# The end of a decoder layer: the second half of the embedding gate's weights is rounded in two pieces, in another order among its neighbours

## The chip, the core and the metric

The kernel runs on one core of a Trainium2 chip. The metric is device time in microseconds (us), the median of several executions. A profiled execution gives the trace: instructions of TensorE (PE, its weight loads as PEld), VectorE (DVE), ScalarE (ACT), GpSimd (POOL) and the queue of SyncE (SP), from which most DMAs are issued. Its span, from the first to the last instruction, is a little shorter than the device time of the same execution.

## The reference, cut to what matters

One layer of a hybrid decoder: two mixers (a gated MLP over chunks and windowed attention), a mixture of 32 experts of which each token takes 4, and an embedding that is added through a gate. There are 512 prompt tokens and 8 sampled ones, 1024 wide.

```python
def layer_forward(h, ple, ...):
    ...
    h = h + mix
    h = h + moe(rmsnorm(h, g_moe)...)          # top 4 of 32 experts
    gate = jax.nn.sigmoid(rmsnorm(h, g_ple) @ w_ple_gate)
    h = h + gate * (ple @ w_ple_proj)
    return h, ...

y = rmsnorm(h, g_final)
```

Inside `moe`, an expert's rows are `clamped_swiglu(xb @ w_gu[e] + b_gu[e]) @ w_dn[e] + b_dn[e]`, and a token's output is the sum of its four rows, each times its gate. `w_ple_gate` is 1024 x 1024, `w_ple_proj` 256 x 1024.

## The kernel before

**Tiles.** Tokens are worked in five tiles: tiles 0 to 3 have 128 prompt tokens each, tile 4 the 8 sampled ones. All products take FP32 operands as a rounded part ("hi") and its remainder ("lo"): hi x hi, hi x lo and lo x hi are summed in a PSUM bank. ScalarE makes the hi part, VectorE the lo part. The eight PSUM banks are `bank[:, 0]` to `bank[:, 7]`.

**Experts.** A loop runs over blocks of up to 128 tokens of one expert; there are 32 blocks, and one more for each time an expert has over 128 tokens (`n_extra`, worked out from the count of tokens for each expert, `total`, line 1541). POOL gathers a block's token rows, ScalarE and VectorE split twelve pieces of weights of 1 MB each, TensorE multiplies, and ScalarE copies the block's output from PSUM into the one buffer `y_sb` (`y_out`, line 1152), from which POOL scatters it to rows in HBM (`store`, line 865). A scatter must have landed before the next `y_out` may write `y_sb`.

**The end.** After the last block (nb - 1) the program is written out by hand, each engine with its own list in order, held together by semaphores:

- `turn_inputs(t)` (PE, L2221, L2224) turns the gate table and the embedding input of tile t; `inputs(t)` copies them out on ACT (L1213, L1214) and DVE (L1692).
- `down_bias(t)` (PE, L2235) multiplies the gates by the experts' output biases into banks 4 and 5; `add_bias(t)` (DVE, L1701) adds them to the residual `h_in`. The two banks are the same for every tile, so `down_bias(t)` waits for `add_bias(t - 1)`.
- `project(t)` (PE, L78 with `wp_hi`, `wp_lo`) is the embedding's projection into banks 6 and 7; `embedding(t)` (ACT, L1220) copies it out. `project(t)` waits for `embedding(t - 1)`.
- `add_experts(t)` (DVE, L1713) adds the four expert rows of each token, which SP loads into `y_in` (L738, L739, L743) once the last scatter has landed. It signals `moe_ready`.
- `turn_f(t)` (PE, L2262) waits for `moe_ready` and turns the tile; `f_hi` (ACT, L1238) and `f_lo` (DVE, L1727) split it; `gate_product(t, w)` (PE, L78 with `wg_hi`, `wg_lo`) multiplies it by half w of the gate's weights; then follow the sigmoid, the embedding and the last norm.
- The gate's weights come in two halves w = 0, 1 of 1024 x 512. `gate_hi(w)` (ACT, L1273) scales and rounds a half in eight instructions, one for each chunk of 128 rows; `split_gate(w)` (DVE, L1753) forms the remainders in eight instructions. `raw` holds the loaded weights.

What TensorE does at the end is, in this order: `turn_inputs` 0 and 1, the last block's down product, then `down_bias(0)`, `turn_inputs` 2 and 3, `project(0)`, `down_bias(1)`, `turn_inputs(4)`, `project(1)`, `down_bias(2)`, `project(2)`, `down_bias(3)`, `project(3)`, `turn_f(0)`, `down_bias(4)`, `project(4)`, and from there for each tile the two gate products with the next tile's `turn_f` between them.

Of the kernel before, what the change touches and what calls it, by code (L numbers as in the profile page):

```python
# [72 lines left out]
def product(nc, out, x_hi, x_lo, w_hi, w_lo, chunks, cols, start, stop):  # L73


    for i, (cx, cw) in enumerate(chunks):
        for j, (a, b) in enumerate(((x_hi, w_hi), (x_hi, w_lo), (x_lo, w_hi))):
            last = nc.tensor.matmul(out, a(cx), b[:, cw, 0:cols], start=start and i == 0 and j == 0,  # L78
                                    stop=stop and i == len(chunks) - 1 and j == 2)
    return last  # L80


def hybrid_layer(nc, x_prompt, x_sample, cache_k, cache_v, p_prompt, p_sample, g_mix, w_in, ln_v_g,
# [10 lines left out]
    KC = D // P  # L94
    HALFK = KC // 2
# [8 lines left out]
    E = w_router.shape[2]  # L104
# [39 lines left out]
    def sem(name):  # L144
        return ctx.enter_context(nc.semaphore(name))
# [9 lines left out]
    bank = ctx.enter_context(nc.psum_tensor("bank", [P, 8, 512], F32))  # L155
# [161 lines left out]
    def scratch(name, shape, dt=F32):  # L317
        nonlocal o
        size = 4
        for n in shape[1:]:  # L320
            size *= n
        t = at(name, shape, dt, o)
        o += -(-size // 32) * 32
        return t
# [89 lines left out]
    total = scratch("total", [P, E])  # L414
# [133 lines left out]
    def piece(b, k):  # L548
        return k if isinstance(b, int) and b == 0 else 12 * b - 4 + k
# [53 lines left out]
    wg_hi_ready, wg_lo_ready, h_biased, emb_ready = sem("wg_hi_ready"), sem("wg_lo_ready"), sem("h_biased"), sem("emb_ready")  # L603
# [8 lines left out]
    def two_banks(b, R):  # L612
        return bank[0:R, b:b + 2, :].rearrange("p b n -> p (b n)")
# [11 lines left out]
    with nc.Block() as block:  # L625
# [263 lines left out]
        def _(act):  # L889
            mine = act_steps.on(act)  # L890
# [255 lines left out]
            def y_out(b, done, first_bank=4):  # L1146

                act.wait_ge(half_used, done)
                if not isinstance(b, int) or b >= 1:
                    act.wait_ge(y_stored, 16 * b)  # L1150
                for s in range(2):
                    last = nc.scalar.activation(y_sb[:, s * CB:(s + 1) * CB], bank[:, first_bank + s, :], ACT.Copy)  # L1152
                last.then_inc(y_ready, 1)
# [51 lines left out]
            def inputs(t):  # L1205

                R, i = ROWS[t], t % NT
                act.wait_ge(turned_in, t + 1)
                if t == NT:
                    act.wait_ge(bdn_done, 1)  # L1210
                    act.wait_ge(ple_proj_done, 1)
                b = bank[:, 2 + t % 2, :]
                nc.scalar.activation(gT[i][:, 0:R], b[0:E, 0:R], ACT.Copy)  # L1213
                nc.scalar.activation(pT_hi[i][:, :, 0:R], b[:, P:P + PC * R].rearrange("p (c r) -> p c r", c=PC),  # L1214
                                     ACT.Copy).then_inc(turned_read, 1)

            def embedding(t):
                R = ROWS[t]
                act.wait_ge(ple_proj_done, t + 1)
                nc.scalar.activation(emb[0:R, t, :], two_banks(6, R), ACT.Copy).then_inc(emb_ready, 1)  # L1220
# [42 lines left out]
                mine.settle()  # L1263
                mine(nc.scalar.activation(st[:, 2:3], st[:, 2:3], ACT.Sqrt, scale=1.0 / D, bias=EPS), out_ss)

            def gate_hi(w):

                if w == 0:
                    act.wait_ge(gain_landed, 80)
                act.wait_ge(raw_landed[w], 48)  # L1270
                act.wait_ge(lo_ready, piece(nb, 1) + 1)
                for c in range(KC):
                    last = nc.scalar.activation(wg_hi[w][:, c, :], raw[w][:, c, :], ACT.Copy, scale=gain_pT[:, c:c + 1])  # L1273
                last.then_inc(wg_hi_ready, 1)

# [2 lines left out]
            y_out(nb - 2, piece(nb - 1, 11) + 1)  # L1278
            act.wait_ge(raw_landed[2], 32)
            nc.scalar.activation(wp_hi[:], wp_raw[:], ACT.Copy).then_inc(wg_hi_ready, 1)  # L1280
            gate_hi(0)
            y_out(nb - 1, piece(nb, 3) + 1, 0)
            inputs(2)
            inputs(3)
            embedding(0)
            gate_hi(1)
            embedding(1)
            inputs(4)
            embedding(2)
            embedding(3)  # L1290
            f_hi(0)
# [12 lines left out]
        def _(dve):  # L1304
            mine = dve_steps.on(dve)
# [232 lines left out]
                                         ALU.subtract), gate_in)  # L1538

            dve.wait_ge(count_done, 1)  # L1540
            mine(nc.vector.tensor_copy(total[:], bank[:, 6, 0:E]))
            mine.settle()
            mine(nc.vector.tensor_scalar(extra[0][:], total[:], float(P), None, ALU.is_gt))
            for j in range(2, -(-TOK // P)):
# [38 lines left out]
            mine = loop_steps  # L1583
# [62 lines left out]
            mine = dve_steps.on(dve)  # L1646
# [13 lines left out]
            mine = loop_steps  # L1660
# [24 lines left out]
            mine = dve_steps.on(dve)  # L1685

            def inputs(t):
                R, i = ROWS[t], t % NT
                dve.wait_ge(turned_read, t + 1)
                if t == NT:  # L1690
                    dve.wait_ge(ple_proj_done, 1)
                mine(nc.vector.tensor_tensor(pT_lo[i][:, :, 0:R],  # L1692
                                             bank[:, 2 + t % 2, P:P + PC * R].rearrange("p (c r) -> p c r", c=PC),
                                             pT_hi[i][:, :, 0:R].bitcast(F32), ALU.subtract), pT_lo_ready)

            def add_bias(t):
                R = ROWS[t]
                if t == 0:
                    dve.wait_ge(h_in_landed, 32)
                dve.wait_ge(bdn_done, t + 1)  # L1700
                mine(nc.vector.tensor_tensor(h_in[0:R, t, :], h_in[0:R, t, :], two_banks(4, R), ALU.add), h_biased)  # L1701
# [44 lines left out]
                mine.settle()  # L1746
                mine(nc.vector.scalar_tensor_tensor(h, h, st[:, 3:4], gain_f[0:R, :], ALU.mult, ALU.mult), y_final)

            def split_gate(w):

                dve.wait_ge(wg_hi_ready, w + 2)
                for c in range(KC):
                    last = nc.vector.scalar_tensor_tensor(wg_lo[w][:, c, :], raw[w][:, c, :], gain_pT[:, c:c + 1],  # L1753
                                                          wg_hi[w][:, c, :].bitcast(F32), ALU.mult, ALU.subtract)
                mine(last, wg_lo_ready)
# [2 lines left out]
            inputs(1)  # L1758
            dve.wait_ge(wg_hi_ready, 1)
            mine(nc.vector.tensor_tensor(wp_lo[:], wp_raw[:], wp_hi[:].bitcast(F32), ALU.subtract), wg_lo_ready)  # L1760
            split_gate(0)
            add_bias(0)
            inputs(2)
            inputs(3)
            add_bias(1)
            inputs(4)
            split_gate(1)
            add_bias(2)
            add_experts(0)
            add_bias(3)  # L1770
# [16 lines left out]
        def _(pe):  # L1787
# [478 lines left out]
            def gate_product(t, w):  # L2266
                if w == 0:
                    pe.wait_ge(fT_hi_ready, t + 1)
                    pe.wait_ge(fT_lo_ready, t + 1)
                    if t == 0:  # L2270
                        pe.wait_ge(y_ready, nb)
                    elif t == 1:
                        pe.wait_ge(h_biased, TILES)
                    else:
                        pe.wait_ge(sg_ready, t - 1)
                if t == 0:
                    pe.wait_ge(wg_lo_ready, w + 2)
                product(nc, bank[:, 4 * (t % 2) + w, :], lambda c: fT_hi[t % 2][:, c, :], lambda c: fT_lo[t % 2][:, c, :],
                        wg_hi[w], wg_lo[w], [(k, k) for k in range(KC)], CB, True, True).then_inc(ple_gate_done, 1)

# [18 lines left out]
            for t in range(TILES):  # L2299
                gate_product(t, 0)  # L2300
                if t + 1 < TILES:
                    turn_f(t + 1)
                gate_product(t, 1)
# [39 lines left out]
```

## Time and profile before

| | us |
|---|---|
| median of 3 runs | 1534.76 (1534.58 to 1535.76) |
| profiled execution | 1534.55 |
| its span | 1533.2 |
| PE busy | 1472.7 (96%) |
| DVE busy | 1229.0 (80%) |
| ACT busy | 1040.3 (68%) |
| POOL busy | 187.5 (12%) |

The shares of busy time are means over the whole span, in which the loop over the experts takes most of the time. The end of the program, from about 1420 us on, has an order and limits of its own; there the rows of a timeline, which give the start and length of each step and the idle time ahead of it, tell more than the shares. Steps of one engine overlap in the rows by up to 0.1 us, as an instruction is counted until its write is through.

### The profile page before, as it was taken

How to read it: one execution, taken by the hardware profiler on the slowest of the kernel's cores; microseconds unless marked ns; L12 is line 12 of the kernel's file. 1: busy time of each engine (PE TensorE's matmuls, PEld its weight loads, DVE VectorE, ACT ScalarE, POOL GpSimd, SP SyncE). 2: the span in 40 equal slices, each digit the busy share in tenths (PEclk: the TensorE clock that was granted, in tenths of full speed). 3: DMA queues.
4: the chain of work that ended last, by engine and by line, in shares of the span. 5: the costliest groups of instructions: out<-in, count | busy, mean ns of one | idle time of the engine just before them, and what ended most of it. 6: DMA issues, size and time to landing. Idle time of an engine off the chain costs nothing.

```text
span 1533.2 us, 21023 instructions
## 1 busy us (share of the span) xinstructions
PE 1472.7 (96%) x6907; PEld 1205.8 (79%) x6907; DVE 1229.0 (80%) x1031; ACT 1040.3 (68%) x980; POOL 187.5 (12%) x237
## 2 busy tenths in 40 slices
PE   5999996799999999999999999999999999999898
PEld 5878775578888888888888888888888888888576
DVE  4246745698888888888888888888888888888775
ACT  4467512377777777777777777777777777777645
POOL 6000013101111111101111111110111111110000
PEclk8999998799999999999999999999999999999999
DMA  9013423899999999999999999999999999998531
GB/s 324 23 65 101 165 84 139 340 338 364 370 368 359 374 366 366 368 368 362 381 375 356 360 367 367 362 362 375 361 379 358 377 356 383 366 360 290 206 127 43
DMA packets 108568, 465.89 MB, mean 304 GB/s; under 512 B 19082, under 2 KB 24722, under 8 KB 75770
## 3 DMA queue, kind: packets, MB, share of 16 engines
q1 hardware_dynamic: 93482, 445.24, 76.6%
q0 software_dynamic: 14432, 18.94, 3.5%
q10 hardware_dynamic: 624, 1.31, 0.3%
q8 instruction: 18, 0.29, 0.1%
q14 instruction: 12, 0.10, 0.0%
HBM read 457.50 MB, written 24.96 MB: 315 GB/s over the span
## 4 chain that ended last, share of the span: by engine, by line
PE 88%; DMA 4%; DVE 3%; ACT 2%; SPq 2%; issue 1%; POOL 0%; POOLq 0%; ACTq 0%; DVEq 0%
PE bank L2151 31%; PE bank L2154 15%; PE bank L2172 15%; PE bank L78 10%; PE bank L2177 7%; PE bank L2143 2%; PE bank L2122 2%; PE bank L2133 2%; DMA v_win<-v_nat 2%; SPq L647 1%; DMA uq<-in_x_prompt 1%; PE bank L1877 1%; PE bank L1847 1%; DMA w_slot<-in_w_dn 1%; PE bank L2069 0%
## 5 line engine op out<-in xcount | busy, mean ns | idle before, releaser
L1588 DVE TENSOR_TENSOR pair_lo<-w_slot,pair_hi 128x2048 fp32r<-128x2048 f32 x384 | 871.3, 2291 | 130.1 <-ACT pair_hi L1123 130.0
L1123 ACT ACTIVATE pair_hi<-w_slot 128x2048 fp32r<-128x2048 f32 x384 | 737.2, 1921 | 268.4 <-PE bank L2154 191.6
L2151 PE MATMUL bank<-pair_hi,xg_hi 128*128 128x512 f32 x1024 | 279.5, 395 | 0.5 <-issue 0.5
L2151 PE MATMUL bank<-pair_hi,xg_lo 128*128 128x512 f32 x1024 | 275.2, 391 | 0.0
L2154 PE MATMUL bank<-pair_lo,xg_hi 128*128 128x512 f32 x1024 | 274.1, 389 | 0.0
L2151 PEld LDWEIGHTS bank<-pair_hi,xg_hi 128*128 128x128 f32 x1024 | 190.7, 189 | 50.8 <-issue 12.8
L2151 PEld LDWEIGHTS bank<-pair_hi,xg_lo 128*128 128x128 f32 x1024 | 193.4, 189 | 40.7
L2154 PEld LDWEIGHTS bank<-pair_lo,xg_hi 128*128 128x128 f32 x1024 | 192.5, 188 | 40.1
L2172 PE MATMUL bank<-pair_hi,aT_hi 128*128 128x512 f32 x496 | 135.7, 395 | 0.0
L2177 PE MATMUL bank<-pair_lo,aT_hi 128*128 128x512 f32 x496 | 133.0, 390 | 0.0
L2172 PE MATMUL bank<-pair_hi,aT_lo 128*128 128x512 f32 x496 | 132.9, 390 | 0.0
L2177 PEld LDWEIGHTS bank<-pair_lo,aT_hi 128*128 128x128 f32 x496 | 93.1, 188 | 20.0
L2172 PEld LDWEIGHTS bank<-pair_hi,aT_lo 128*128 128x128 f32 x496 | 93.1, 188 | 19.9
L2172 PEld LDWEIGHTS bank<-pair_hi,aT_hi 128*128 128x128 f32 x496 | 90.8, 188 | 17.0
L78 PE MATMUL bank<-half_hi,xT_hi 128*128 128x512 f32 (+1 forms) x220 | 86.3, 392 | 4.6 <-DVE half_lo L254 2.8
L78 PE MATMUL bank<-half_hi,xT_lo 128*128 128x512 f32 (+1 forms) x220 | 83.0, 377 | 0.0
L78 PE MATMUL bank<-half_lo,xT_hi 128*128 128x512 f32 (+1 forms) x220 | 82.9, 377 | 0.0
L846 POOL DMA_INDIRECT xg<-hn_rows,idx_in x33 | 37.0, 1120 | 320.9 <-PE bank L2122 283.3
L865 POOL DMA_INDIRECT expert_rows<-y_sb,idx_out x32 | 44.2, 1382 | 210.5 <-ACT y_sb L1152 137.3
L1144 ACT ACTIVATE gate_sb<-bank 128x512 f32<-128x512 f32 x64 | 34.8, 596 | 35.1 <-PE bank L2154 35.1
L855 POOL DMA_DIRECT2D bias_sb<-bias_rows x32 | 19.7, 614 | 289.9 <-issue 252.7
L78 PEld LDWEIGHTS bank<-half_hi,xT_hi 128*128 128x128 f32 x220 | 42.3, 192 | 14.1 <-issue 3.9
(305 smaller groups left out, 1460.7 us busy)
## 6 DMA issues: line engine op xcount, KB each, us to landing
w_slot<-in_w_gu SPq DMA_DIRECT2D x256, 1024.0 KB, 6.5
w_slot<-in_w_dn SPq DMA_DIRECT2D x128, 1024.0 KB, 6.1
raw<-in_w_in SPq DMA_DIRECT2D x3, 2048.0 KB, 22.8
y_in<-expert_rows SPq DMA_DIRECT2D x3, 2048.0 KB, 10.1
raw<-in_w_o SPq DMA_DIRECT2D x2, 2048.0 KB, 8.7
raw<-in_w_ple_gate SPq DMA_DIRECT2D x2, 2048.0 KB, 10.9
uq<-in_x_prompt SPq DMA_DIRECT2D x4, 512.0 KB, 7.7
x_rows<-in_x_prompt SPq DMA_DIRECT2D x4, 512.0 KB, 6.8
```

The lines of the kernel that those rows point to most:

```text
L78: last = nc.tensor.matmul(out, a(cx), b[:, cw, 0:cols], start=start and i == 0 and j == 0, stop=stop and i == len(chunks) - 1 and j == 2)
L846: pool.indirect_dma_start(xg[:], None, hn_rows, bass.IndirectOffsetOnAxis(idx_in[:, 0:1], 0), bounds_check=last_token, oob_is_err=False).t ...
L865: pool.indirect_dma_start(expert_rows, bass.IndirectOffsetOnAxis(idx_out[:, 1:2], 0), y_sb[:], None, bounds_check=last_row, oob_is_err=Fal ...
L1123: nc.scalar.activation(pair_hi[pair(b, k)][:], w_slot[k + down][:], ACT.Copy).then_inc(hi_ready, 1)
L1144: nc.scalar.activation(gate_sb[:, p * CB:(p + 1) * CB], bank[:, p, :], ACT.Gelu_apprx_sigmoid).then_inc(gate_ready, 1)
L1588: mine(nc.vector.tensor_tensor(pair_lo[pair(b, k)][:], w_slot[k + down][:], pair_hi[pair(b, k)][:].bitcast(F32), ALU.subtract), lo_ready)
L2122: last = nc.tensor.transpose(bank[:, 6 + c // 4, (c % 4) * P:(c % 4 + 1) * P], xg[:, c * P:(c + 1) * P], ident[:])
L2133: last = nc.tensor.transpose(bank[:, 6 + p, c * P:(c + 1) * P], acts[:, p * CB + c * P:p * CB + (c + 1) * P], ident[:])
L2151: nc.tensor.matmul(bank[:, n, :], x[:, c, :], w_hi[:, n * CB:(n + 1) * CB], start=False, stop=False)
L2154: last = nc.tensor.matmul(bank[:, n, :], xg_hi[:, c, :], w_lo[:, n * CB:(n + 1) * CB], start=False, stop=c == KC - 1)
L2172: nc.tensor.matmul(bank[:, first_bank + s, :], a[:, 2 * j + i, :], w_hi[:, i * D + s * CB:i * D + (s + 1) * CB], start=j == 0 and i == 0 a ...
L2177: last = nc.tensor.matmul(bank[:, first_bank + s, :], aT[0][:, 2 * j + i, :], w_lo[:, i * D + s * CB:i * D + (s + 1) * CB], start=False, s ...
```

## The change

The second half of the gate's weights (w = 1) is rounded, and its remainders are formed, in two pieces of four chunks each. On ScalarE the first piece stands ahead of the copy of the last block's rows (`y_out(nb - 1)`) and the second behind `inputs(3)`; `inputs(4)` goes ahead of `embedding(1)`. On VectorE the first piece stands ahead of `add_bias(1)` and the second behind it, so that `add_bias(2)` and `add_experts(0)` follow `inputs(4)`. The semaphore `wg_lo_ready` counts one more step, which the gate's product waits for. Besides, the count of tokens for each expert is read from bank 1, into which TensorE writes it (`positions`), instead of bank 6, in which the last tile's router logits stand.

```diff
-            def gate_hi(w):
+            def gate_hi(w, chunks):
...
-                for c in range(KC):
+                for c in chunks:
                     last = nc.scalar.activation(wg_hi[w][:, c, :], raw[w][:, c, :], ACT.Copy, scale=gain_pT[:, c:c + 1])
                 last.then_inc(wg_hi_ready, 1)
...
-            gate_hi(0)
+            gate_hi(0, range(KC))
+            gate_hi(1, range(HALFK))
             y_out(nb - 1, piece(nb, 3) + 1, 0)
             inputs(2)
             inputs(3)
+            gate_hi(1, range(HALFK, KC))
             embedding(0)
-            gate_hi(1)
+            inputs(4)
             embedding(1)
-            inputs(4)
             embedding(2)
...
-            mine(nc.vector.tensor_copy(total[:], bank[:, 6, 0:E]))
+            mine(nc.vector.tensor_copy(total[:], bank[:, 1, 0:E]))
...
-                dve.wait_ge(wg_hi_ready, w + 2)
-                for c in range(KC):
+                dve.wait_ge(wg_hi_ready, w + 1 + chunks.stop // HALFK if w else 2)
+                for c in chunks:
...
-            split_gate(0)
+            split_gate(0, range(KC))
             add_bias(0)
             inputs(2)
             inputs(3)
+            split_gate(1, range(HALFK))
             add_bias(1)
+            split_gate(1, range(HALFK, KC))
             inputs(4)
-            split_gate(1)
             add_bias(2)
...
-                    pe.wait_ge(wg_lo_ready, w + 2)
+                    pe.wait_ge(wg_lo_ready, 2 * w + 2)
```

How the program's instructions stand on ScalarE between the rounding of the first half (`wg_hi_190`, eight chunks of `raw_49`) and the first tile's `f_hi` (`fT_hi_208`), before (-) and now (+); `wg_hi_191` is the second half, `y_sb` the copy of the last rows, `gT` and `pT_hi` are the inputs, `emb` the projections:

```order
 L1273 ACTIVATE wg_hi_190<-raw_49,gain_pT 128x512 x8
+L1273 ACTIVATE wg_hi_191<-raw_50,gain_pT 128x512 x4
 L1150 REGISTER_ALU
 L1152 ACTIVATE y_sb<-bank 128x512 x2
...
 L1213 ACTIVATE gT_223<-bank 32x128
 L1214 ACTIVATE pT_hi_215<-bank 128x256
-L1220 ACTIVATE emb<-bank 128x1024
-L1273 ACTIVATE wg_hi_191<-raw_50,gain_pT 128x512 x8
+L1273 ACTIVATE wg_hi_191<-raw_50,gain_pT 128x512 x4
 L1220 ACTIVATE emb<-bank 128x1024
 L1213 ACTIVATE gT_220<-bank 32x8
 L1214 ACTIVATE pT_hi_212<-bank 128x2x8
-L1220 ACTIVATE emb<-bank 128x1024 x2
+L1220 ACTIVATE emb<-bank 128x1024 x3
```

Four of the eight roundings of the second half now stand ahead of the copy into `y_sb`, four ahead of the first `emb`, and the inputs of tile 4 stand behind one `emb` instead of two.

VectorE before, from the remainders of the first half (`wg_lo_192`) to the bias sum of tile 3; `h_in<-h_in,bank` is `add_bias`, `pT_lo` the inputs, `h_in<-y_in_202,gates,h_in` `add_experts(0)`:

```order
L1753 SCALAR_TENSOR_TENSOR wg_lo_192<-raw_49,gain_pT,wg_hi_190 128x512 x8
L1701 TENSOR_TENSOR h_in<-h_in,bank 128x1024
L1692 TENSOR_TENSOR pT_lo_218<-bank,pT_hi_214 128x256
L1692 TENSOR_TENSOR pT_lo_219<-bank,pT_hi_215 128x256
L1701 TENSOR_TENSOR h_in<-h_in,bank 128x1024
L1692 TENSOR_TENSOR pT_lo_216<-bank,pT_hi_212 128x2x8
L1753 SCALAR_TENSOR_TENSOR wg_lo_193<-raw_50,gain_pT,wg_hi_191 128x512 x8
L1701 TENSOR_TENSOR h_in<-h_in,bank 128x1024
L1713 SCALAR_TENSOR_TENSOR h_in<-y_in_202,gates,h_in 128x1024 x4
L1701 TENSOR_TENSOR h_in<-h_in,bank 128x1024
```

The same stretch of VectorE now (the lines of this half of the program are numbered one higher):

```order
L1754 SCALAR_TENSOR_TENSOR wg_lo_192<-raw_49,gain_pT,wg_hi_190 128x512 x8
L1702 TENSOR_TENSOR h_in<-h_in,bank 128x1024
L1693 TENSOR_TENSOR pT_lo_218<-bank,pT_hi_214 128x256
L1693 TENSOR_TENSOR pT_lo_219<-bank,pT_hi_215 128x256
L1754 SCALAR_TENSOR_TENSOR wg_lo_193<-raw_50,gain_pT,wg_hi_191 128x512 x4
L1702 TENSOR_TENSOR h_in<-h_in,bank 128x1024
L1754 SCALAR_TENSOR_TENSOR wg_lo_193<-raw_50,gain_pT,wg_hi_191 128x512 x4
L1693 TENSOR_TENSOR pT_lo_216<-bank,pT_hi_212 128x2x8
L1702 TENSOR_TENSOR h_in<-h_in,bank 128x1024
L1714 SCALAR_TENSOR_TENSOR h_in<-y_in_202,gates,h_in 128x1024 x4
L1702 TENSOR_TENSOR h_in<-h_in,bank 128x1024
```

The eight remainders of the second half stood between `add_bias(1)` and `add_bias(2)`, behind the inputs of tile 4; now four stand ahead of `add_bias(1)` and four directly behind it.

## Rows read from the trace of the kernel before

**Rows 1.** The page: the span and the count of instructions.
```profile
span 1533.2 us, 21023 instructions
```

**Rows 2.** Busy us by stretch; its length, busy (x instructions), granted clock, DMA share, GB/s.
```profile
1422.00:1448.60 26.60, 26.48 (x105) 18.28 (x105) 18.51 (x23) 18.78 (x34) 2.72 (x3) 1.00 0.53 194
1448.60:1452.30 3.70, 0.00 (x0) 0.00 (x0) 3.62 (x5) 1.02 (x1) 0.00 (x0) 0.86 1.02 414
1452.30:1461.50 9.20, 9.14 (x17) 5.36 (x18) 6.27 (x5) 0.00 (x0) 0.00 (x0) 0.50 0.31 108
1473.70:1525.60 51.90, 51.85 (x243) 42.59 (x241) 35.62 (x42) 29.77 (x47) 0.00 (x0) 1.00 0.21 80
```

**Rows 3.** Chain that ended last, from 1439 us: start, length, what (merged pieces).
```profile
1439.56 4.13 ACT wg_hi L1273 x7
...
1445.79 5.30 DVE wg_lo L1753 x8
1451.09 1.14 DVE h_in L1701
...
1456.11 5.43 PE bank L78 x12
```

**Rows 4.** Timeline of TensorE: start, length, instruction xcount, [idle before <-releaser].
```profile
1433.10 1.98 PE L2235 MATMUL bank<-b_down,gT 32*128 32x512 f32 x4
1435.01 0.28 PE L2221 MATMUL bank<-ident,gate_table 128*32 128x128 f32 x1
...
1435.59 0.47 PE L78 MATMUL bank<-wp_hi,pT_hi 128*128 128x512 f32 x1
...
1438.53 1.98 PE L2235 MATMUL bank<-b_down,gT 32*128 32x512 f32 x4
...
1443.54 1.98 PE L2235 MATMUL bank<-b_down,gT 32*128 32x512 f32 x4
...
1452.36 3.75 PE L2235 MATMUL bank<-b_down,gT 32*128 32x512 f32 x4 [3.78 <-DVE h_in L1701]
...
1461.33 1.14 PE L2262 MATMUL bank<-ident,h_in 128*128 128x128 f32 x8
...
1472.85 1.10 PE L2262 MATMUL bank<-ident,h_in 128*128 128x128 f32 x8 [0.19 <-DVE h_in L1713]
```

**Rows 5.** Timeline of ScalarE: first half rounded, last rows' copy, end of inputs(3).
```profile
1426.79 5.00 ACT L1273 ACTIVATE wg_hi<-raw,gain_pT 128x512 fp32r<-128x512 f32 x8
1434.23 1.09 ACT L1152 ACTIVATE y_sb<-bank 128x512 f32<-128x512 f32 x2 [2.44 <-DMA expert_rows<-y_sb,idx_out]
...
1436.14 0.36 ACT L1214 ACTIVATE pT_hi<-bank 128x256 fp32r<-128x256 f32 x1
```

**Rows 6.** Timeline of GpSimd: the last block's index rows and scatter.
```profile
1434.86 0.55 POOL L860 DMA_DIRECT2D idx_out<-slot_table  x1 [7.81 <-DMA expert_rows<-y_sb,idx_out]
1437.62 1.02 POOL L865 DMA_INDIRECT expert_rows<-y_sb,idx_out  x1 [2.21 <-DMA idx_out<-slot_table]
```

**Rows 7.** Timeline of VectorE from the first half's remainders on.
```profile
1431.82 5.39 DVE L1753 SCALAR_TENSOR_TENSOR wg_lo<-raw,gain_pT,wg_hi 128x512 fp32r<-128x512 f32 x8 [2.61 <-ACT wg_hi L1273]
1437.13 1.22 DVE L1701 TENSOR_TENSOR h_in<-h_in,bank 128x1024 f32<-128x1024 f32 x1
1438.26 0.75 DVE L1692 TENSOR_TENSOR pT_lo<-bank,pT_hi 128x256 fp32r<-128x256 f32 x2
...
1452.32 5.31 DVE L1713 SCALAR_TENSOR_TENSOR h_in<-y_in,gates,h_in 128x1024 f32<-128x1024 f32 x4
```

**Rows 8.** DMA issues from 1440.89, 1441.82 and 1391.3 us: xcount, KB, us to landing.
```profile
y_in<-expert_rows SPq DMA_DIRECT2D x1, 1024.0 KB, 5.4
...
y_in<-expert_rows SPq DMA_DIRECT2D x1, 2048.0 KB, 12.1
...
raw<-in_w_ple_gate SPq DMA_DIRECT2D x1, 2048.0 KB, 13.3
```

**Rows 9.** Line 865, all scatters: shortest/median/longest ns, first and last start us.
```profile
L865 POOL DMA_INDIRECT expert_rows<-y_sb,idx_out x32: 1021/1512/2788, 350.6 to 1437.6; - x32
```

More of the change, by code:

```diff
@@ L1747, in norm_out, with split_gate @@
                 mine(nc.vector.scalar_tensor_tensor(h, h, st[:, 3:4], gain_f[0:R, :], ALU.mult, ALU.mult), y_final)
-            def split_gate(w):
-                dve.wait_ge(wg_hi_ready, w + 2)
-                for c in range(KC):
+            def split_gate(w, chunks):
+                dve.wait_ge(wg_hi_ready, w + 1 + chunks.stop // HALFK if w else 2)
+                for c in chunks:
                     last = nc.vector.scalar_tensor_tensor(wg_lo[w][:, c, :], raw[w][:, c, :], gain_pT[:, c:c + 1],
```

## The prediction

> **What bounds the kernel now.** Read the page first: a span of 1533.2 us [rows 1], of which the loop over the experts is the largest part. The diff leaves that loop alone; it works on the last 100 us, so the views to read are those of the stretch from 1422 us. The table by stretch [rows 2] shows TensorE busy for 26.48 of 26.60 us up to 1448.6, then not at all for 3.70 us, then busy at a granted clock of 0.50, which is 1.2 GHz, for 9.2 us, and from 1473.7 on busy for 51.85 of 51.90 us at 1.00 (2.4 GHz). So the end is one long TensorE chain with a single hole in it, and behind the hole a slow stretch. Whatever removes the hole moves everything behind it, since the five gate products that follow have no room left between them.
>
> What made the hole stands in the chain of waits [rows 3]: ScalarE rounds the second half of the gate's weights (wg_hi, 4.13 us of it on the chain), VectorE forms their remainders in one run of eight (5.30 us), then the bias sum of tile 2 (1.14 us), and only then TensorE may start down_bias(3), whose two banks that sum has to empty first. TensorE's rows say the same: down_bias(3) starts at 1452.36 after 3.78 us of idling for VectorE's h_in [rows 4]. Nobody on TensorE needs these remainders then; the first user is gate_product(0, 1), behind turn_f(1) at 1472.85 [rows 4]. They are merely queued in front of add_bias(2).
>
> **The change part by part.**
>
> *ScalarE, first piece ahead of the last rows' copy.* Eight roundings take 5.00 us [rows 5], so four take 2.5. They start where the eight of the first half end, at 1431.79 or up to 0.1 before it (neighbours overlap that much in the rows), and end near 1434.25. The copy y_out(nb - 1) has its idle time of 2.44 us exactly there, and starts at 1434.23 because the rows before it leave y_sb only then [rows 5]. So the copy is late by 0 to 0.1 us. What if it were later? Behind it stands POOL's scatter, which also waits for its index rows: these are asked for at 1434.86, and POOL then idles 2.21 us for them until the scatter goes at 1437.62 [rows 6]. The copy takes 1.09 us and ends at 1435.32, so up to 2.3 us of delay reach nobody. The weights themselves landed 13.3 us after an issue before 1392 [rows 8], so this piece waits for no transfer. Cost: nothing.
>
> *ScalarE, second piece behind inputs(3).* inputs(3) ends at 1436.50; four roundings end near 1438.95, and embedding(0), for which project(0) is done at 1435.59 + 2.94 = 1438.5 [rows 4], comes 0.3 us later than now, ending near 1439.9. project(1) needs it; it starts at about 1440.5, behind down_bias(1) (1438.53 + 1.98) and the last transposes [rows 4]. 0.6 us of room: nothing. In return embedding(1) no longer stands behind eight roundings and inputs(4) no longer behind embedding(1).
>
> *VectorE.* It is busy without a gap from 1431.82, so its steps can be laid end to end, with durations from [rows 7]: the eight remainders of the first half end at 1437.2, add_bias(0) at 1438.35, inputs(2) and inputs(3) at 1439.0. Now four remainders: 5.39 us for eight, so 2.7 for four, to 1441.7; add_bias(1) (1.22 less 0.1 of overlap) to 1442.8; four more to 1445.5; the small inputs(4) to 1445.6; add_bias(2) to 1446.8, against 1452.2; add_experts(0), 5.31 us, to 1452.1, against 1457.6; add_bias(3) to 1453.3.
>
> Two of these release TensorE at another time than now. add_bias(1) is later by some of the four remainders ahead of it, and down_bias(2) waits for it; that starts at 1443.54 [rows 4], so 0.7 us of room are left: nothing. add_bias(2) is 5.4 us earlier (1452.23 now [rows 3]), and down_bias(3) finds its banks empty when project(2) is done.
>
> *TensorE.* The hole goes. From 1443.54 the steps follow each other at full clock: down_bias takes 1.91 us to the next step's start (1433.10 to 1435.01), a projection 2.94 us (1435.59 to 1438.53) [rows 4], 4.85 together. So turn_f(0), two such pairs behind 1443.54, starts at 1453.24. It starts at 1461.33 now [rows 4]. The gain is 8.09 us: 3.8 of idling, the rest the half clock over down_bias(3) (3.75 us against 1.98) and project(3) (5.43 us against 2.94) [rows 3, 4]. The slowest reading of the rows is the pair from 1438.53 to 1443.54, 5.01 us, which has the small transposes in it; by it the gain is 7.77.
>
> *Who is late next?* turn_f(0) also needs moe_ready, the end of add_experts(0) at 1452.1: 1.1 us of room. That step in turn needs the gathered rows, which used to be there long before. Their first megabyte lands 5.4 us after 1440.89, at 1446.3, and it is wanted at 1446.8. The last of the three transfers in the queue lands 12.1 us after 1441.82, at 1453.9 [rows 8]. The second megabyte is not seen landing; as 1 of the 3 MB that come between 1446.3 and 1453.9 it should land near 1448.8 if the queue keeps its order, and it is wanted by the third sum, near 1449.4. If the two transfers in the queue shared evenly, it would land near 1451.5, add_experts(0) would end at 1454.1 and turn_f(0) would lose 0.9. I take the order of the queue, since the first landing agrees with it, and keep 7.2 as the lower end of the gain.
>
> *The rest* (the gate's product waits for semaphore value 4 instead of 3, the count is read from bank 1) is one instruction for one instruction. From turn_f(0) on, ScalarE's and VectorE's steps all hang on project(3) and turn_f(0) and move with them; the gate products are bound by TensorE [rows 2], and so the end moves by the same 8.1 us.
>
> *A rule of the Trainium skill.* Its page "GPSIMD Engine Reference" (1. Specifications) says that GpSimd's SBUF interfaces are shared with VectorE, and that they collide with VectorE instructions that have two SBUF inputs; the remainders are such instructions. In this trace the scatters of expert rows took 1.02 to 2.79 us [rows 9], and the last one, beside add_bias(0), 1.02 [rows 6]. If the last scatter fell into the moved remainders and took the longest of these times, the rows would land 1.8 us later, add_experts(0) would end near 1453.4, and the sum would be 7.9 instead of 8.1. The remainders start at 1439.0 and the scatter is issued by 1438.64, so I leave it out.
>
> **The rivals.**
>
> *The rows come too late.* The room of 1.1 us in front of turn_f(0) is what the forecast lives on. If the gathered rows come d us later than laid out, d - 1.1 is lost; and if the new hole grows to some 3.7 us, the clock falls again and the following 9 us run at half speed, as they do now. Then the hole has only moved behind project(3). Time: between 1527 and 1534.5. For it: the second megabyte's landing was not seen. Against it: the first was, in time, and nothing ahead of it moves.
>
> *The clock falls anyway.* If the half clock at 1452 came not from the hole but from the light work before it (small transposes, products over 32 rows), the hole would go and the slow stretch stay: gain 3.8, time 1531.0. Against it: that same light work ran at 1.00 from 1433 to 1448.6 [rows 2], and the clock was lower only behind the hole.
>
> *Nothing reaches the end.* This needs a second bound behind the hole, as late as the first. The rows show a TensorE chain without a gap behind 1473.7, so little speaks for it: 1533.5 to 1535.
>
> *Slower: another expert block.* The count of tokens for each expert was read from a bank in which the logits stand; read from the bank with the counts, it can exceed 128. From one expert with 129 tokens on, the loop runs a 33rd time. A block costs (1437.6 - 350.6) / 31 = 35.1 us [rows 9], so the time would be 1534.8 + 35.1 - 8.1 = 1561.8. Against it: 520 tokens in four choices over 32 experts are 65 for each on average, and the reference's own routing, worked out for its inputs, gives at most 117.
>
> **How the numbers follow.** The profiled execution took 1534.55 us, 0.2 below the median of 1534.76. 1534.76 - 8.1 = 1526.66. Chances: the forecast (1525.8 to 1527.8) 0.80; rows too late 0.09, half of it within 2.5 us of the forecast; clock falls anyway 0.04; nothing reaches the end 0.04; slower block or anything else that costs 0.03. The range from 1525.7 to 1529.2 takes in the lower end of the gain (7.2, so 1527.6) and the smaller part of the first rival. A measurement of this kernel tells 0.2% (3.1 us) from no change. By that: faster 0.91, same 0.06, slower 0.03.
>
> **What would show it.** Right: TensorE without a hole at 1448 to 1453, granted clock 1.00 from 1422 to the end of the products, add_bias(2) ending near 1446.8, turn_f(0) near 1453.2, the last gate product ending near 1517.5, and y_out still near 1434.3 with its idle time gone. Wrong: idle time of TensorE in front of turn_f(0) or project(1), VectorE waiting for y_in inside add_experts(0), the last scatter later than 1438, or 33 blocks.

## The result, and the profile after

| | before | changed |
|---|---|---|
| median, us | 1534.58 (5 runs, 1533.39 to 1535.76) | 1526.15 (5 runs, 1525.64 to 1526.72) |
| ratio | | 0.9945, 95% interval 0.993 to 0.9959 |
| profiled execution, us | 1534.55 | 1526.72 |
| its span, us | 1533.2 | 1525.3 |

8.4 us less (0.55%; the interval reaches from 6.3 to 10.7), where 8.1 were forecast.

The part ahead of the change differs from execution to execution: the first multiplication of the last block's down product starts between 1421.0 and 1427.0 us in the profiles of this study, all of them with the same program up to there except for the bank that the count is read from. So beside the times each kernel is read by its **end stretch**, from that multiplication to the end of the span: 111.2 us before (from 1422.00), 102.9 changed (from 1422.37), 8.3 us less. An end stretch is that of one profiled execution; the times are those of all executions and contain the part ahead. The changed kernel's rows stand 0.37 us later than those of before from this alone.

The stretches of the changed kernel (columns as in [rows 2]: busy us of TensorE, its weight loads, VectorE, ScalarE, GpSimd; the hole and the slow stretch behind it have no counterpart any more):

```profile
1422.00:1448.60 26.60, 26.23 (x105) 18.31 (x105) 23.72 (x30) 19.13 (x34) 2.71 (x3) 1.00 0.50 183
1448.60:1453.30 4.70, 4.70 (x17) 2.84 (x16) 4.56 (x4) 1.02 (x1) 0.00 (x0) 1.00 0.99 403
1453.30:1465.40 12.10, 11.88 (x54) 8.29 (x53) 8.10 (x9) 5.96 (x9) 0.00 (x0) 1.00 0.48 178
1465.40:1517.60 52.20, 52.20 (x247) 43.08 (x245) 35.52 (x41) 30.19 (x46) 0.00 (x0) 1.00 0.20 78
```

TensorE's granted clock is 1.00 (2.4 GHz) throughout. It is busy but for 0.37 us at the start of the first row, where this execution is not yet at its down product, and 0.22 us in front of turn_f(1). The hole and the 9.2 us at 0.50 are gone. In the chain of waits (start, length, what) the pieces of ScalarE and VectorE of [rows 3] have gone with them; up to turn_f(0) the pairs of bias product and projection stand end to end:

```profile
1443.98 1.91 PE bank L2237 x4
1445.89 2.95 PE bank L78 x12
1448.84 1.91 PE bank L2237 x4
1450.75 2.97 PE bank L78 x12
```

VectorE (beside [rows 7]): the four remainders, add_bias(2), add_experts(0), add_bias(3) follow each other without a wait.

```profile
1443.08 2.74 DVE L1754 SCALAR_TENSOR_TENSOR wg_lo<-raw,gain_pT,wg_hi 128x512 fp32r<-128x512 f32 x4
...
1445.93 1.22 DVE L1702 TENSOR_TENSOR h_in<-h_in,bank 128x1024 f32<-128x1024 f32 x1
1447.25 5.32 DVE L1714 SCALAR_TENSOR_TENSOR h_in<-y_in,gates,h_in 128x1024 f32<-128x1024 f32 x4
1452.48 1.22 DVE L1702 TENSOR_TENSOR h_in<-h_in,bank 128x1024 f32<-128x1024 f32 x1
```

ScalarE (beside [rows 5]): twelve roundings in a row, and 0.36 us of the 2.44 are left in front of the copy, since the rows before it left `y_sb` a little later in this execution.

```profile
1427.17 7.45 ACT L1273 ACTIVATE wg_hi<-raw,gain_pT 128x512 fp32r<-128x512 f32 x12
1434.98 1.08 ACT L1152 ACTIVATE y_sb<-bank 128x512 f32<-128x512 f32 x2 [0.36 <-DMA expert_rows<-y_sb,idx_out]
```

GpSimd's last scatter, then TensorE's turn_f(0) and turn_f(1) (beside [rows 4, 6]):

```profile
1438.37 1.02 POOL L865 DMA_INDIRECT expert_rows<-y_sb,idx_out  x1 [2.21 <-DMA idx_out<-slot_table]
```
```profile
1453.54 1.04 PE L2264 MATMUL bank<-ident,h_in 128*128 128x128 f32 x8
...
1465.00 1.09 PE L2264 MATMUL bank<-ident,h_in 128*128 128x128 f32 x8 [0.22 <-DVE h_in L1714]
```

The scatter still waits 2.21 us for its index rows, so nothing of the moved roundings reached it. turn_f(0) follows project(3) without a wait.

### The profile page after: what moved, and what is told of

It is laid out like the page before. It is cut to its first block, busy times and chain, and to the rows that moved or that the text cites. A ratio compares the mean times of both kernels' runs of the same rounds, so it can differ in the third digit from the quotient of the medians.

```text
span 1525.3 us, 21024 instructions
## 1 busy us (share of the span) xinstructions
PE 1467.7 (96%) x6907; PEld 1204.2 (79%) x6907; DVE 1228.9 (81%) x1031; ACT 1040.3 (68%) x980; POOL 187.2 (12%) x237
## 4 chain that ended last, share of the span: by engine, by line
PE 89%; DMA 4%; DVE 3%; ACT 2%; SPq 2%; issue 1%; POOL 0%; POOLq 0%; DVEq 0%; ACTq 0%
PE bank L2153 31%; PE bank L2156 15%; PE bank L2174 15%; PE bank L78 10%; PE bank L2179 7%; PE bank L2145 2%; PE bank L2124 2%; DMA v_win<-v_nat 2%; PE bank L2135 2%; SPq L647 1%; DMA uq<-in_x_prompt 1%; PE bank L1879 1%; PE bank L1849 1%; DMA w_slot<-in_w_dn 1%; PE bank L2237 1%
## 6 DMA issues: line engine op xcount, KB each, us to landing
raw<-in_w_ple_gate SPq DMA_DIRECT2D x2, 2048.0 KB, 10.7
```

## The experiments

Theory: the gain is the hole in front of down_bias(3) and the half clock behind it, and the room of 1 us in front of turn_f(0) is what carries it. The rivals are those of the prediction, and a question it left unasked: which of the two engines' orders made the hole.

The idling in the table is TensorE's in front of a bias product or turn_f(0); the 0.2 us in front of turn_f(1), which the kernel before has too, are left out. The time at clock 0.50 is counted from the end of that idling to the last gate product.

| kernel | idling of TensorE on the way, us | at clock 0.50, us | end stretch, us | ratio to before (95%) |
|---|---|---|---|---|
| before | 3.78 | 9.2 | 111.2 | 1 |
| changed | none | none | 102.9 | 0.9945 (0.993 to 0.9959) |
| changed_again | none | none | 103.0 | 0.9952 (0.9938 to 0.9965) |
| act_only | 0.44 | 3.4 | 104.9 | 0.9954 (0.9941 to 0.9967) |
| act_only_again | 0.41 | none | 103.6 | one execution |
| dve_only | 2.55 | 3.4 | 107.1 | 0.9987 (0.9978 to 0.9996) |
| hole2 | 0.86 | 3.4 | 105.5 | 0.9969 (0.9958 to 0.998) |
| hole2_again | 0.82 | 3.4 | 105.4 | one execution |
| hole5 | 4.59 | 8.5 | 111.7 | 1.0004 (0.9993 to 1.0014) |
| count_only | 3.78 | 6.8 | 110.1 | 1.0009 (1.0 to 1.0018) |
| eight_ahead | none | none | 102.9 | 0.9961 (0.9948 to 0.9974) |
| halves_swapped | 0.91 | none | 104.1 | 0.9972 (0.9962 to 0.9983) |
| tile1_first | 3.50 | 9.4 | 110.6 | 1.0 (0.9991 to 1.0009) |
| sums_before_norm | none | none | 102.5 | 0.9946 (0.9933 to 0.996) |

### Which engine's order made the hole

`act_only`, ScalarE's order of the change with VectorE's of before:

```diff
-            split_gate(1, range(HALFK))
             add_bias(1)
-            split_gate(1, range(HALFK, KC))
             inputs(4)
+            split_gate(1, range(HALFK))
+            split_gate(1, range(HALFK, KC))
             add_bias(2)
```

> ScalarE in the order of the change, VectorE in the order of before (all eight remainders of the second half behind the inputs of tile 4, ahead of add_bias(2)). Theory A: the hole came from ScalarE, whose late rounding of the second half kept the inputs of tile 4 back, so that VectorE idled 3.85 us for them ahead of its remainders. Then VectorE now runs through: inputs(4) near 1442.2, remainders to 1447.5, add_bias(2) to 1448.7, just when TensorE is free for down_bias(3) (1448.8), so no hole and no half clock; add_experts(0) ends near 1454.1 and turn_f(0) is 0.6 us later than with the whole change: about 1526.8. Theory B: the hole came from VectorE's order, the run of eight ahead of add_bias(2). Then it stays, and the time is 1533 to 1534.6.

VectorE of `act_only` (the cut row is inputs(4)), and below it the row of the kernel before that the prediction passed over, VectorE's inputs(4):

```profile
1444.54 1.22 DVE L1702 TENSOR_TENSOR h_in<-h_in,bank 128x1024 f32<-128x1024 f32 x1 [1.55 <-PE bank L2237]
...
1445.76 5.38 DVE L1754 SCALAR_TENSOR_TENSOR wg_lo<-raw,gain_pT,wg_hi 128x512 fp32r<-128x512 f32 x8
1451.06 1.21 DVE L1702 TENSOR_TENSOR h_in<-h_in,bank 128x1024 f32<-128x1024 f32 x1
```

Before:

```profile
1445.61 0.17 DVE L1692 TENSOR_TENSOR pT_lo<-bank,pT_hi 128x16 fp32r<-128x16 f32 x1 [3.85 <-ACT pT_hi L1214]
```

Before, VectorE stood idle for 3.85 us, because inputs(4) was queued on ScalarE behind the eight roundings and embedding(1). With ScalarE's order alone that wait is gone, the run of eight remainders stays whole, and add_bias(2) ends at 1452.27, when TensorE asks for its banks at 1452.41. Theory A: the hole is gone, with 0.44 us left in front of turn_f(0). Behind these 0.44 us the profiled execution lost 1.4 us more than expected, to a half clock (below). `act_only` moves the first roundings and inputs(4) together; which of the two was needed, no run tells.

`dve_only` is the other half: VectorE's order of the change, ScalarE's of before.

```diff
-            gate_hi(1, range(HALFK))
             y_out(nb - 1, piece(nb, 3) + 1, 0)
             inputs(2)
             inputs(3)
-            gate_hi(1, range(HALFK, KC))
             embedding(0)
-            inputs(4)
+            gate_hi(1, range(HALFK))
+            gate_hi(1, range(HALFK, KC))
             embedding(1)
+            inputs(4)
```

> VectorE in the order of the change (four remainders ahead of add_bias(1), four behind it), ScalarE in the order of before (second half rounded behind embedding(0), inputs(4) behind embedding(1)). Theory A: VectorE now waits for the first four roundings until 1442.5, so add_bias(1) ends near 1446.4 and TensorE idles 2.5 us ahead of down_bias(2); add_bias(2) follows near 1450.3 without a further hole, and if 2.5 us of idling leave the clock at 1.00, turn_f(0) comes near 1456: about 1528.7. Theory B: the order on VectorE is what matters: about 1526.2.

```profile
1445.76 2.15 PE L2237 MATMUL bank<-b_down,gT 32*128 32x512 f32 x4 [2.55 <-DVE h_in L1702]
```
```profile
1441.74 2.74 DVE L1754 SCALAR_TENSOR_TENSOR wg_lo<-raw,gain_pT,wg_hi 128x512 fp32r<-128x512 f32 x4 [3.09 <-ACT wg_hi L1273]
```

TensorE's hole moved one step ahead, to down_bias(2), 2.55 us where 2.5 were forecast, because VectorE waits 3.09 us for roundings that are not there yet; another 1.6 us went to a half clock. Of the 8.3 us of the end stretch this order alone gives 4.1 in its profile, ScalarE's alone 6.3 and 7.6 in two. They are not two gains to be added: each order alone leaves a hole of its own, in another place and of another length. The times agree with this for `act_only` (7.1 us less than before, 5.1 to 9.1). For `dve_only` they are 2.0 us less (0.6 to 3.4), so its profile, the fastest of twelve executions, shows more than they do; what the others lost was not seen.

### The hole and the clock

`hole2` and `hole5` put two and five subtractions of 128x1024 ahead of add_bias(2) of the changed kernel:

```diff
             inputs(4)
+            for i in range(5):
+                mine.settle()
+                mine(nc.vector.tensor_tensor(sg[:], wg_hi[0][:, 0:2, :].bitcast(F32), wg_hi[0][:, 2:4, :].bitcast(F32), ALU.subtract))
             add_bias(2)
```

> The changed kernel with five such subtractions ahead of add_bias(2), about 6.3 us, so that TensorE idles some 4.7 us, one more than in the kernel before. Theory: the hole and the half clock belong together; down_bias(3) and project(3) run at 1.2 GHz again (9 us instead of 4.8) and turn_f(0) is about 9 us later: about 1535. Rival (the half clock of before had another cause, which the change took away): only the idling comes back and add_experts(0) decides, turn_f(0) 5.4 us later: about 1531.6, clock 1.00.

```profile
1454.53 3.75 PE L2240 MATMUL bank<-b_down,gT 32*128 32x512 f32 x4 [4.59 <-DVE h_in L1702]
```
```profile
1449.95:1454.50 4.55, 0.00 (x0) 0.00 (x0) 4.38 (x5) 1.02 (x1) 0.00 (x0) 0.82 0.88 353
1454.50:1463.20 8.70, 8.67 (x16) 5.09 (x17) 6.26 (x5) 0.00 (x0) 0.00 (x0) 0.51 0.23 73
```

A hole of the old kind brings back down_bias(3) at 3.75 us, a stretch at 0.51 and 8.8 us of the end. That the hole and the half clock belong together is shown: TensorE did the same work, in the same order, in the changed kernel at 1.00. `hole5` also gives VectorE 6 us more to do; `tile1_first` (below) makes a hole without that, and the clock falls there too.

> The changed kernel with two extra subtractions of 128x1024 on VectorE (about 1.25 us each, their output not used) ahead of add_bias(2). If idling costs only itself while it is short: TensorE idles 0.9 us ahead of down_bias(3), then add_experts(0) ends 2.5 us later, 1.5 us behind the room in front of turn_f(0): about 1527.7, granted clock 1.00 throughout. If any idling halves the clock: 1530 to 1532, with clock 0.50 behind 1450.

```profile
1450.64 1.95 PE L2240 MATMUL bank<-b_down,gT 32*128 32x512 f32 x4 [0.86 <-DVE h_in L1702]
```
```profile
1450.60:1453.00 2.40, 2.36 (x6) 1.10 (x7) 2.36 (x2) 0.25 (x1) 0.00 (x0) 0.98 1.03 413
1453.20:1456.60 3.40, 3.40 (x10) 2.68 (x9) 3.26 (x4) 0.00 (x0) 0.00 (x0) 0.54 0.31 122
1456.80:1468.40 11.60, 11.39 (x50) 7.81 (x48) 7.94 (x9) 5.54 (x9) 0.00 (x0) 1.00 0.46 182
```

The end is 2.6 us longer, not 1.5: 0.86 us of idling in front of down_bias(3), and then, 2.3 us behind it, the clock falls for 3.4 us while TensorE is busy. So a short hole costs more than its length here. Is that always so?

> The kernel with two extra subtractions ahead of add_bias(2), once more. It took 105.5 us over the end, 2.6 more than the changed kernel, with 3.4 us at 0.50 behind 0.86 us of idling. If the drop belongs to the idling: 105.5 again. If it is a matter of the execution: down to 104.4 without it.

> The kernel with only ScalarE's order changed, once more. It took 104.9 us over the end where 103.5 was expected: behind 0.44 us of idling in front of turn_f(0) the clock was 0.50 for 3.4 us. If that drop belongs to the idling, it comes again: 104.9. If a short idle time only loses the clock in some executions: 103.5 or 104.9.

`hole2_again` lost the clock again (105.4 us). `act_only_again` didn't. turn_f(0) and the stretch behind it in `act_only` and, under it, in `act_only_again`:

```profile
1457.74 1.09 PE L2264 MATMUL bank<-ident,h_in 128*128 128x128 f32 x8 [0.44 <-DVE h_in L1714]
```
```profile
1457.20:1460.80 3.60, 3.04 (x14) 1.17 (x13) 2.43 (x4) 2.95 (x5) 0.00 (x0) 0.99 0.47 135
1460.90:1464.30 3.40, 3.40 (x9) 2.68 (x10) 2.04 (x4) 1.58 (x4) 0.00 (x0) 0.53 1.01 414
```
```profile
1457.62 1.09 PE L2264 MATMUL bank<-ident,h_in 128*128 128x128 f32 x8 [0.41 <-DVE h_in L1714]
```
```profile
1457.10:1460.70 3.60, 3.06 (x14) 1.19 (x13) 2.43 (x4) 2.97 (x5) 0.00 (x0) 1.00 0.47 139
1460.80:1464.20 3.40, 3.40 (x15) 2.77 (x16) 2.04 (x4) 2.02 (x4) 0.00 (x0) 1.00 1.01 417
```

The same program, with the same idling within 0.03 us: once at 0.53 and once at 1.00 behind it. So whether a short hole in this part of TensorE's work (transposes, products over 32 rows, a projection) loses the clock differs from execution to execution, and its length alone doesn't decide it: `halves_swapped` (below) kept the clock behind 0.91 us. The idling can be counted on, the 3.4 us at half clock can't. In the four profiles without such a hole (changed, changed_again, eight_ahead, sums_before_norm) the clock stayed at 1.00 until the products were over.

### The count

`count_only` is the kernel before with the changed line of the count alone.

```diff
-            mine(nc.vector.tensor_copy(total[:], bank[:, 6, 0:E]))
+            mine(nc.vector.tensor_copy(total[:], bank[:, 1, 0:E]))
```

> The kernel before with nothing but the count of tokens read from bank 1. If no expert has over 128 tokens: 32 blocks and the time of before, within 0.7 us. If one has (the slower rival): 33 scatters and 35 us more, 1569.7.

```profile
L865 POOL DMA_INDIRECT expert_rows<-y_sb,idx_out x32: 1022/1548/3027, 352.3 to 1439.4; - x32
```

32 scatters, so 32 blocks, and a ratio of 1.0009 (1.0 to 1.0018, 0 to 2.8 us more): the slower rival's 35 us did not come about, and the line gives none of the gain. This run also shows what the half clock of before is worth from one execution to the next: behind the same hole of 3.78 us, down_bias(3) and project(3) took 8.00 us here (1453.73 to 1461.73) and 8.97 in [rows 4].

```profile
1453.73 3.71 PE L2235 MATMUL bank<-b_down,gT 32*128 32x512 f32 x4 [3.78 <-DVE h_in L1701]
```
```profile
1453.70:1461.70 8.00, 7.97 (x16) 4.55 (x17) 6.26 (x5) 0.00 (x0) 0.00 (x0) 0.57 0.28 82
```

Read in steps of 0.2 us, the clock was at 0.50 from 1453.8 to 1460.6 here, so it fell just as the hole ended; before, it fell some 1.1 us ahead of the hole's end and stayed there until 1461.5.

### The copy, the scatter and the rows

`eight_ahead` rounds the whole second half ahead of the last rows' copy.

```diff
             gate_hi(1, range(HALFK))
+            gate_hi(1, range(HALFK, KC))
             y_out(nb - 1, piece(nb, 3) + 1, 0)
             inputs(2)
             inputs(3)
-            gate_hi(1, range(HALFK, KC))
             embedding(0)
```

> The changed kernel with all eight roundings of the second half ahead of the last rows' copy. Theory: the copy is 2.1 us later (about 1437.1) and still hidden behind the index rows of the last scatter, which stays near 1438.4, so the time is that of the change, 1526.2 within 0.5. Rival (the copy is on the path to the scatter): scatter and y_in 2 us later, of which 1 us is covered ahead of turn_f(0): 1527.2 to 1528.2.

```profile
1442.14 1.02 POOL L865 DMA_INDIRECT expert_rows<-y_sb,idx_out  x1 [2.68 <-ACT y_sb L1152]
```
```profile
1442.61 2.73 DVE L1754 SCALAR_TENSOR_TENSOR wg_lo<-raw,gain_pT,wg_hi 128x512 fp32r<-128x512 f32 x4
...
1450.95 1.28 DVE L1714 SCALAR_TENSOR_TENSOR h_in<-y_in,gates,h_in 128x1024 f32<-128x1024 f32 x1 [0.49 <-DMA y_in<-expert_rows]
```

The scatter now waits for the copy instead of its index rows and is 0.45 us later against the end stretch's beginning; VectorE waits 0.49 us for the rows; turn_f(0) is where it was, and the end stretch is 102.9. So the room is there, in both places, and a little of it was used. The expectation was off by that 0.45, which it had as nothing. Its time of 1526.2 was missed as well: the median is 1529.04, beside 1534.48 for the kernel before, 6.0 us less (4.0 to 8.0), which can't be told from the changed kernel's 8.4. These rows also show the moved remainders beside the scatter, from 1442.61 to 1443.16: it took 1.02 us, as it does without them.

`halves_swapped` loads the second megabyte of tile 0's rows first.

```diff
-            sp.dma_start(y_in[0][:, 0:2, :], y_by_token[0:P, 0:2, :]).then_inc(y_first_landed, 16)
             sp.dma_start(y_in[0][:, 2:TOPK, :], y_by_token[0:P, 2:TOPK, :]).then_inc(y_in_landed[0], 16)
+            sp.dma_start(y_in[0][:, 0:2, :], y_by_token[0:P, 0:2, :]).then_inc(y_first_landed, 16)
```

> The changed kernel, with the second megabyte of the gathered rows of tile 0 loaded ahead of the first, so that the sums begin only when both are there. If the queue keeps its order: the first two rows land about 2.5 us later than now (near 1449.5 instead of 1447.05), VectorE waits 2.3 us for them, and behind 1.0 us of room turn_f(0) is 1.3 us later: about 1527.5, no half clock. If the two transfers share the queue, or the room is larger: 1526.2.

```profile
1447.93 5.31 DVE L1714 SCALAR_TENSOR_TENSOR h_in<-y_in,gates,h_in 128x1024 f32<-128x1024 f32 x4 [2.09 <-DMA y_in<-expert_rows]
```
```profile
1453.30 1.09 PE L2264 MATMUL bank<-ident,h_in 128*128 128x128 f32 x8 [0.91 <-DVE h_in L1714]
```

The second of the two transfers lands 7.1 us after its issue at 1440.78, where the first, in the changed kernel, landed after 5.4: here the transfers land one after the other, in the order of their issue. This landing comes 2.0 us behind where the first megabyte is wanted in the changed kernel. VectorE waits 2.09 us, 0.91 of it come through to turn_f(0), 1.1 us to the end. No half clock here, behind 0.91 us of idling. The timed runs lose more than this one profile (4.3 us less than before, 2.6 to 5.8, where the profile's end gives 7.1). The profiled execution was the fastest of ten, with the part ahead at its shortest (1421.04). That some of the others lost the clock, as `act_only` did once, would fit too, but was not seen; this stays open.

`tile1_first` goes further and puts tile 1's 2 MB ahead of tile 0's.

```diff
+            sp.dma_start(y_in[1][:], rows_of(y_by_token, 1)).then_inc(y_in_landed[1], 16)
             sp.dma_start(y_in[0][:, 0:2, :], y_by_token[0:P, 0:2, :]).then_inc(y_first_landed, 16)
             sp.dma_start(y_in[0][:, 2:TOPK, :], y_by_token[0:P, 2:TOPK, :]).then_inc(y_in_landed[0], 16)
-            for t in range(1, TILES):
+            for t in range(2, TILES):
```

> The changed kernel, with the 2 MB of tile 1's rows loaded ahead of tile 0's: the first rival (rows too late) on purpose. The rows of tile 0 land 5 us later, near 1452, add_experts(0) ends near 1457.4 and TensorE idles 3.9 us ahead of turn_f(0). Theory: the clock falls to 0.50 there, the hole has moved behind project(3): 1533 to 1534.4. Rival (only the idling costs): 1530.1, clock 1.00.

```profile
1456.60 1.97 PE L2265 MATMUL bank<-ident,h_in 128*128 128x128 f32 x8 [3.50 <-DVE h_in L1715]
```
```profile
1456.60:1465.60 9.00, 9.00 (x21) 4.76 (x22) 5.55 (x7) 3.61 (x6) 0.00 (x0) 0.50 0.62 233
```

The whole gain is gone (end stretch 110.6, ratio 1.0): the prediction's first rival, made on purpose, with the hole moved behind project(3) and 9.4 us at half clock behind it. Tile 0's first megabyte lands 10.3 us after its issue at 1440.94, against the end stretch's beginning 4.8 us later than in the changed kernel.

### One more move

`changed_again` repeats the changed kernel. `sums_before_norm` moves one wait more: in the changed kernel turn_f(1) idles 0.22 us for add_experts(1), which VectorE forms behind a wait for tile 0's norm.

```diff
-            norm_in(0)
             add_bias(4)
             add_experts(1)
+            norm_in(0)
```

> The changed kernel once more, beside the next three. From the first multiplication of the last block's down product to the end of the span it took 102.9 us, with the granted clock at 1.00 all the way to the last gate product. If the clock there is safe without a hole: 102.9 again within 0.3. If the light stretch from 1452 to 1460 can lose it without a hole: up to 2 us more.

> The changed kernel with one more move on VectorE: add_bias(4) and add_experts(1) go ahead of the reciprocal of tile 0's norm, for which VectorE waits 1.26 us behind ScalarE's table load; only the sigmoid, 13 us later, needs it. turn_f(1), which now idles 0.22 us for add_experts(1), then starts when TensorE is free: 102.5 to 102.7 over the end instead of 102.9. If something else holds turn_f(1): 102.9. Slower would mean that the sigmoid waits for the reciprocal.

```profile
1466.14 1.03 PE L2264 MATMUL bank<-ident,h_in 128*128 128x128 f32 x8
```

The changed kernel's end was 103.0 us again, at clock 1.00. With the move, turn_f(1) starts at 1466.14, 11.1 us behind turn_f(0) instead of 11.5, without a wait, and the end stretch is 102.5. It is the fastest of all ends here; by the times (1526.75 against 1527.64 us, side by side) 0.5 us can't be told from nothing.

## Why the prediction was right

- *The bound.* TensorE's chain with one hole and a slow stretch behind it: right; `hole5` puts both back and the 8.8 us with them.
- *The sum.* 8.09 us to turn_f(0); measured 1461.33 - 1453.54, plus the 0.37 by which this execution was late at the start, 8.16. A pair of bias product and projection took 4.86 and 4.77 us, forecast 4.85. To the end it is 8.3, since turn_f(0) itself took 1.04 us instead of 1.14. It is these rows that bear the sum out; the times alone, 8.4 us with an interval from 6.3 to 10.7, couldn't tell 8.1 from 7.
- *ScalarE's first piece at no cost.* Right; `eight_ahead` shows that 2.1 us more would have cost the scatter 0.45 and the end nothing. One sign of being wrong did come up: the last scatter started at 1438.37, later than 1438. It was not the roundings, which left 0.36 us of idling in front of the copy: of the 0.75 us by which it is later than in [rows 6], 0.37 are this execution's late start and the rest the later landing of the rows before.
- *add_bias(1) later, with 0.7 us of room.* Right, down_bias(2) came without a wait.
- *The room in front of turn_f(0).* Forecast 1.1 us; add_experts(0) ended at 1452.57 and turn_f(0) started at 1453.54, so 0.97. In front of the first sum it was less than thought: the rows landed 5.4 us after 1441.65, at 1447.05, and were wanted at 1447.25. The second megabyte, by the 7.1 us of `halves_swapped`, came at 1449.2 and was wanted at 1449.9. The order of the queue, which was taken over equal shares, held.
- *GpSimd's shared interfaces.* The rule of the Trainium skill ("GPSIMD Engine Reference", 1. Specifications) was left out of the sum. In the changed kernel the scatter ended 0.09 us after the moved remainders began, so they hardly met; in `eight_ahead` they overlapped for 0.55 us and the scatter took 1.02 us all the same, so no price of it is seen in this overlap.
- *The cause of the hole* was put in the wrong place, without harm to the sum. The prediction read it as remainders queued ahead of add_bias(2), and took VectorE as busy without a gap from 1431.82. In the kernel before it was not: it idled 1.53 us in front of add_bias(1) and 3.85 in front of inputs(4). `act_only` leaves the remainders there, and the hole is gone: the 3.85 us were VectorE's wait for inputs(4), which ScalarE had queued behind its roundings. The prediction named that move in half a sentence and gave it no price.
- *"The clock falls anyway"* had a chance of 0.04, on the ground that light work had run at 1.00. For the changed kernel that held in both its profiles. But light work behind a short hole did lose the clock in some executions (`act_only`, `hole2`), so the rival was nearer than the text had it: the changed kernel leaves no hole up to turn_f(0), and short ones there are not harmless.

## What to carry to other kernels

When an engine idles in front of the bound one, follow its own idle rows back one step further: the wait of 3.85 us on VectorE, behind work on ScalarE whose result TensorE first used 29 us later, was the root, and moving that work into idle times which other waits had already made was free. A hole on TensorE between light steps is worth closing to the end: here 0.4 to 0.9 us of it could be followed by 3.4 us at half clock (1.3 to 1.7 us more), and was in three profiles of five. Where a gain rests on a room of a microsecond, know what lands last ahead of it; here 4.8 us of delay in a queue of DMAs took the whole gain back.

## What was not expected of the hardware

- The granted clock fell from 1.00 to 0.50 for 3.4 us some 2.5 us behind an idle time of 0.82 to 0.86 us (`hole2` and `hole2_again`) and about 3 us behind one of 0.44 us (`act_only`, not `act_only_again`), while TensorE was busy with transposes, products over 32 rows and a projection; behind 0.91 us in `halves_swapped` it stayed at 1.00. Behind 2.55 us (`dve_only`) it was at 0.50 for 3.4 us. Behind idle times of 3.5 to 4.6 us it was at 0.50 for 6.8 to 9.4 us in all four profiles (before, `count_only`, `hole5`, `tile1_first`).
- The same hole of 3.78 us cost 8.00 us over the two steps behind it in one execution and 8.97 in another.
